# The silu behind a layer norm written to PSUM instead of SBUF, and an output projection whose first pass covers three column tiles instead of four

## The reference, cut to what matters

```
a, gl, z = split(u @ w_in, 3)
v = a * sigmoid(gl)
y = depthwise_conv(v, width 31) + b_dw
y = silu(layernorm(y, g_ln, b_ln))       # mean and variance over the 1024 channels
out = (y * silu(z)) @ w_out              # 1024 x 1024
h = h + rmsnorm(out, g_post)
```

## Time and profile before

| | us |
|---|---|
| median of 3 runs | 633.22 |
| lowest and highest run | 632.15, 635.92 |
| the profiled execution's own time | 633.14 |
| its span, first to last instruction | 631.4 |
| busy over the span: PE, DVE, ACT, POOL | 545.7, 451.3, 306.8, 298.2 |

### The profile page before, as it was taken

The page is one execution under the profiler, slowest core; times in us unless marked ns, Lnnn a source line. Parts: engine busy times, 40 slices in busy tenths (PEclk is TensorE's granted clock), DMA queues, the critical chain, the costliest instruction groups (busy, mean ns, idle before and its releaser), DMA issues.

```text
span 631.4 us, 10827 instructions
## 1 busy us (share of the span) xinstructions
PE 545.7 (86%) x4044; PEld 497.4 (79%) x4044; DVE 451.3 (71%) x855; ACT 306.8 (49%) x730; POOL 298.2 (47%) x271
## 2 busy tenths in 40 slices
PE   0699999999983669998999998998999999779981
PEld 0699999988952669987999997777777777469980
DVE  4887999999987994888758122856867868850066
ACT  5454665365646773655336325355454554444230
POOL 3349878898894770473647731102111112205033
PEclk9999999999997689999999999999999999959996
DMA  7233133222430310332133222020030031101003
GB/s 239 82 104 89 52 103 90 79 76 66 136 86 1 103 31 28 88 95 67 34 101 105 95 83 57 15 72 17 13 91 2 17 120 36 49 17 51 2 30 112
DMA packets 31397, 43.17 MB, mean 68 GB/s; under 512 B 5840, under 2 KB 21744, under 8 KB 31344
## 3 DMA queue, kind: packets, MB, share of 16 engines
q1 hardware_dynamic: 31344, 42.47, 23.2%
HBM read 37.25 MB, written 3.10 MB: 64 GB/s over the span
## 4 chain that ended last, share of the span: by engine, by line
PE 42%; DVE 36%; ACT 6%; issue 5%; POOL 4%; SPq 3%; DMA 3%; DVEq 0%; ACTq 0%; POOLq 0%
DVE ps L957 13%; PE ps L421 10%; PE ps L423 9%; PE ps L422 9%; PE ps L1636 3%; PE ps L1677 2%; DVE probs L1209 2%; POOL part L1288 2%; DVE y L1002 2%; PE ps L1657 2%; DVE ps L871 2%; SPq L484 2%; ACT probs L787 2%; POOL rlow_lo L412 1%; DVE y L854 1%
## 5 line engine op out<-in xcount | busy, mean ns | idle before, releaser
L412 POOL TENSOR_TENSOR rlow_lo<-stage,rlow_hi 128x384 fp32r<-128x384 f32 (+2 forms) x88 | 99.6, 1141 | 215.8 <-ACT rlow_hi L406 215.8
L421 PE MATMUL ps<-act_hi,rlow_hi 128*128 128x272 f32 (+1 forms) x368 | 110.7, 301 | 22.0 <-POOL act_lo L1341 9.3
L957 DVE SCALAR_TENSOR_TENSOR ps<-v,vecs,ps 128x574 f32<-128x574 f32 x165 | 120.6, 814 | 0.0
L421 PE MATMUL ps<-act_hi,rtop_hi 128*128 128x272 f32 x384 | 112.8, 294 | 7.7 <-ACT zs L627 4.0
L423 PE MATMUL ps<-act_hi,rtop_lo 128*128 128x272 f32 x384 | 111.7, 291 | 0.0
L422 PE MATMUL ps<-act_lo,rtop_hi 128*128 128x272 f32 x384 | 111.3, 290 | 0.0
L423 PE MATMUL ps<-act_hi,rlow_lo 128*128 128x272 f32 (+1 forms) x368 | 107.9, 293 | 0.0
L422 PE MATMUL ps<-act_lo,rlow_hi 128*128 128x272 f32 (+1 forms) x368 | 107.8, 293 | 0.0
L421 PEld LDWEIGHTS ps<-act_hi,rlow_hi 128*128 128x128 f32 (+1 forms) x368 | 70.4, 191 | 25.6 <-POOL act_lo L1341 10.6
L421 PEld LDWEIGHTS ps<-act_hi,rtop_hi 128*128 128x128 f32 x384 | 73.0, 190 | 9.1 <-ACT zs L627 4.3
L412 POOL TENSOR_TENSOR rtop_lo<-stage,rtop_hi 128x384 fp32r<-128x384 f32 (+1 forms) x56 | 64.8, 1177 | 28.4 <-ACT rtop_hi L406 28.4
(11 more groups left out here) (180 smaller groups left out, 1254.9 us busy)
## 6 DMA issues: line engine op xcount, KB each, us to landing
stage<-w_in SPq DMA_DIRECT2D x64, 192.0 KB, 2.7
stage<-w_bi SPq DMA_DIRECT2D x24, 256.0 KB, 2.7
stage<-w_ao SPq DMA_DIRECT2D x16, 256.0 KB, 2.9
stage<-w_bo SPq DMA_DIRECT2D x16, 256.0 KB, 2.7
stage<-w_qb SPq DMA_DIRECT2D x16, 192.0 KB, 2.6
xT<-x_t SPq DMA_DIRECT2D x4, 544.0 KB, 5.5
y_out<-xT SPq DMA_DIRECT2D x16, 136.0 KB, 1.8
stage<-w_kb SPq DMA_DIRECT2D x8, 256.0 KB, 2.6
```

The costliest lines, as they stand in the source:

```text
L412: nc.gpsimd.tensor_tensor(l, stage[:, u % STAGES, 0:unit_cols(u)], h.bitcast(F32), ALU.subtract).then_inc(lo_done, 1)
L421: nc.tensor.matmul(out, wh, xh, start=start, stop=False)
L957: ins = nc.vector.scalar_tensor_tensor(out=dst, in0=src, scalar=tap, in1=dst, op0=ALU.mult, op1=ALU.add)
```

## The change

The silu writes into one of two PSUM banks, taken in turn, and the gate reads it there; its other operand (`zs`) and its output (`y`) stay in SBUF. The banks are 6 and 3 in block 0 and 6 and 7 in block 1. The silu of step n waits for the gate of step n - 2, which read the bank before. Bank 6 is no longer free for the reciprocal of block 1, so both blocks use bank 5, and the second reciprocal waits until the eight normalisations of block 0 are done. Bank 3 is no longer free for output tile 3 during the first pass, so this pass covers tiles 0 to 2 (nine matmuls for each k), and tile 3 comes behind it as a tile of its own, without a wait for an evacuation.

```
-LNB = (5, 6)
+LN_RSTD = 5
+SILU_BANKS = ((6, 3), (6, 7))
+O_FIRST = 3
...
+        def silu_out(n):
+
+            b, k = divmod(n, KD)
+            return ps[:, SILU_BANKS[b][k % 2], 0:HB]
...
                 act.wait_ge(ln_norm, n + 1)
-                nc.scalar.activation(y[:, k, blk(b)], y[:, k, blk(b)], ACT.Silu, bias=vecs[:, V_BLN + k:V_BLN + k + 1],
+                if n >= 2:
+                    act.wait_ge(yz_full, n - 1)
+                nc.scalar.activation(silu_out(n), y[:, k, blk(b)], ACT.Silu, bias=vecs[:, V_BLN + k:V_BLN + k + 1],
...
-                bank = {N_IN: 4, N_IN + 1: 5, N_LN: LNB[0], N_LN + 1: LNB[1], N_O[0]: 4, N_O[1]: 5,
+                bank = {N_IN: 4, N_IN + 1: 5, N_LN: LN_RSTD, N_LN + 1: LN_RSTD, N_O[0]: 4, N_O[1]: 5,
...
-                nc.vector.tensor_tensor(y[:, k, blk(b)], y[:, k, blk(b)], zs[:, k, blk(b)], ALU.mult).then_inc(yz_full, 1)
+                nc.vector.tensor_tensor(y[:, k, blk(b)], silu_out(n), zs[:, k, blk(b)], ALU.mult).then_inc(yz_full, 1)
...
                 if n == KD:
+                    dve.wait_ge(ln_norm, KD)
                     inverse(N_LN + 1, None, 1)
...
-                for m in range(4):
+                for m in range(O_FIRST):
...
-            for n in range(4, 2 * KD):
+            for n in range(O_FIRST, 2 * KD):
                 b, m = divmod(n, KD)
-                pe.wait_ge(o_evac, n - 3)
+                if n >= 4:
+                    pe.wait_ge(o_evac, n - 3)
```

## The result

The changed kernel takes **630.63 us** (median of 17 runs, 628.33 to 632.33). The kernel before takes 635.76 (17 runs in all, with the three known earlier; 631.89 to 637.27). The ratio is 0.9933, with a 95% interval of 0.9918 to 0.9949: faster by 0.5 to 0.8%. The medians lie 5.13 apart; the forecast was a gain of 4.87.

The account below looks back on a forecast made before the run. DVE's gate and POOL were taken to hold each other up, leaving PE idle before tile 4. Gains of 3.25 (tile 4's earlier start) and 1.62 (clock) sum to 4.87 off 633.14, giving 628.3; range 626.0 to 631.5.

Parts of the forecast that it names:

- The gate reads PSUM: DVE's sixteen gates: each falls from 1.02 to 0.43 us, the centring's time, shedding 9.4 on DVE, not itself the gain.
- POOL late next, 1.99 a step: POOL in block 0: rests shorten by 0.2, steps go from 2.19 to 1.99, the eighth rest ends 1.6 earlier.
- The first pass over three tiles: PE's output projection: pass ends at 224.9, tile 3 then takes 3.02 alone, a price covered by PE's wait for bank 0.
- Tile 4's wait and the clock: PE at output tile 4: starts at 227.9 instead of 231.15, gaining 3.25; without the clock's fall, a further 1.62.
- the dip: Granted clock falling to 1.2 GHz behind PE's idle gap before tile 4; its removal was priced at 1.62.
- Silu into PSUM and the new waits: ACT's silu writes and the added waits: taken as costing nothing; the write's bounds were -0.05 to +0.22 each.
- The lead carried on: From tile 5 to the end: all of the lead is passed on; the other bound was that it is lost.
- The rival of the thinner pass: PE's clock falls in the nine-matmul pass: tile 3 cold costs 2.4, gain 2.5, 630.7; chance 0.14.
- How the numbers follow: Chances for the whole run: 0.16 faster by over one per cent (6.3 us), 0.81 within it, 0.03 slower.
- one dip fewer: Rival: arriving earlier at later low-clock stretches avoids one more dip, worth 1.62, giving 626.7; chance 0.14.
- the low clock: Rival: clock falls in the thinner pass (gain 2.5) or the old dip returns at tile 4 (gain 3.25); chance 0.14.
- The base: Starting time of the forecast: profiled execution's 633.14, 0.08 below the median of 633.22.

Follow-up runs that it names:

- e3: Kernel before with only the gate's second operand changed, to a reciprocal already in PSUM, leaving silu(z) out of the result: 626.25 us, ratio 0.9883.
- e6: e4 with every odd rest (low part of y) moved from POOL to DVE: 631.13 us, ratio 0.9949 to the kernel before.
- e7: e4 with the tail's scaling on DVE taken through PSUM: 621.34 us, ratio 0.9785 to the kernel before.
- e4: Changed kernel with one silu bank instead of two and four tiles in the first pass again: 627.45 us, ratio 0.9895 to the kernel before.
- e8: e4 once more, unedited, on the chip of e5 to e7: 627.31 us, ratio 0.9871 to the kernel before.
- e5: Changed kernel with one silu bank instead of two, first pass still over three tiles: 629.24 us, ratio 0.9916 to the kernel before.
- e2: Kernel before with only the first pass cut to three tiles, silu and gate left in SBUF: 632.89 us, ratio 0.9971.
- e1: The changed kernel run again with no edit, for a second profile: 630.01 us, ratio 0.9935 to the kernel before.

## Why the prediction was right, and where it was wrong

*The gate reads PSUM: right.* 0.437 where 0.43 was said. e3 shows that the operand alone does it, e6 and e7 that it holds for other instructions and in both directions. One reading was off: the rest that takes 0.76 at 230.60 does not run beside fewer gates. A gate starts inside it, at 230.68, and takes 0.98. What spared this rest is that it began first (see the last section). The Trainium skill, "SBUF — State Buffer", section "Who interferes with whom", says that a DVE instruction with two SBUF inputs contends with a GpSimd instruction that reads SBUF, and that one with at most one SBUF input, outside the two-port modes, does not. The trace agrees: 1020 ns against 437 for the gate, and 0.97 against 0.77 for the rest beside it.

*POOL late next, 1.99 a step: right.* Measured 1.97; the eighth rest ended 0.17 sooner than said. e6 supports it: where every second rest is taken off POOL, the last rest of block 0 ends 1.0 sooner.

*The first pass over three tiles: right in its price.* Tile 4 followed at 18.87 behind the first rest; 18.94 was said (227.9 - 208.96). The sentence that PE's wait for bank 0 covers this price described the kernel before. With the gate repaired no such wait is left: in e4, with four tiles and `evac_o(0)` at 227.09, PE does not wait for it. The prediction took the three tiles as given and did not ask what the gate alone would bring. That is 2.6 more (e4 and e8 against e5).

*Tile 4's wait and the clock: right.* No idle time ahead of tile 4, 1.00 from 218 on, 3.32 and a further 1.57 up to tile 6's evacuation (3.25 and 1.62 were said). e2 separates the two: 1.54 for the dip alone.

*Silu into PSUM and the new waits: right.* 0.577 on average against 0.607, so the write costs nothing, as taken. The row of 0.38 that served as a copy from PSUM for its lower bound is the square (line 626); the sum does not use it. e4 and e5 wait even more strictly at no cost.

*The lead carried on: right as far as it can be seen.* 4.89 at tile 6 and 4.88 at attention's start (4.79 in e1). At the tail's table load it is 5.00 in the profile after (395.99 and 390.99 behind the first rest) and 3.87 in e1's (392.12): there the scatter of the stretch between is as large as what is looked for. The medians lie 5.13 apart, and 4.40 in e1.

*The rival of the thinner pass: fell.* Four of the eight groups of nine put it to the test. The first four ran at the low clock from the start and left PE no wait, as the prediction says of a cold pass. Ahead of each of the last four PE idled 0.46 to 0.59, and the clock stayed at 1.00 from 218 on; in e1 and e5, with idle times of 0.56 to 0.59, it stayed there too. By the Trainium skill, "TensorE: Matmul & The Clock Gate", section "A second HAM failure mode: psum-queue depth-cycling", short idles between groups can make it swing; here four in a row did not.

*How the numbers follow: this is the step that failed.* The time and its cause were as forecast, and the ratio of 0.9933 lies within one per cent, the case that had 0.81. But the text called one per cent, 6.3 us, about what a measurement of this kernel can tell from no change, and so its likeliest case read as a change that makes no difference. The runs say otherwise: the interval of 0.9918 to 0.9949 is 1.0 us to either side, and the whole of it lies on the faster side. A gain of 5.13 is there and can be told from none, although it is less than one per cent. Even e2, 1.5 us below, could be told from no change (0.9951 to 0.9991). With that bound the chance of a gain that can be seen was the forecast's 0.59 (4.87 us), 0.14 (one dip fewer, 6.5) and 0.14 (the low clock, 2.5 to 3.25): 0.87 in place of 0.16. The bound of 6.3 was a round share of the time, six times what the repeated runs leave open and more than the spread of the three runs on hand (632.15 to 635.92); it had not been set against the size of the move.

*The base.* The forecast of 628.3 lies 2.3 below the 630.63 measured, although the gain was right within 0.3. The three runs' median of 633.22 was 2.5 below that of all 17, and the base was taken from them; for that reason the result lies above the forecast's own 627.5 to 630.0, though inside the whole range. Two short series of sums that take 2.56 to 4.90 and 2.1 to 3.7 from one profile to the next, and the 229.45 to 232.99 from attention's start to the tail, are of that size; that they make the scatter of the runs was not measured.

## What to carry to other kernels

Where DVE and POOL work at once, look for DVE instructions with both inputs in SBUF that take longer beside POOL than alone, and let the step ahead of them write one operand to PSUM; both engines get quicker. Test such a repair by itself before anything is rearranged around it: here the second half of the change gave back 2.6 us of what the first had won, and the same repair in the tail was worth another 6.0. And price a gain against the interval that repeated runs give, not against a round share of the time, and don't take the base from three runs.

## What the runs showed that was not expected

The granted clock of a short series of matmuls can differ between two executions of one program with the same idle time ahead: in the kernel after the sums of y had 0.50 in one profile and 1.00 in the next, both behind 2.08 of idle time, and the last sums took 3.74 and 2.10 behind 2.32. That was worth 2.1 and 1.6 us, so a difference of that size between two single profiles of this kernel can be that alone. It is no rare event here: with about the same idle time ahead, the sums of y ran at the high clock throughout in three of the ten profiles (before, e1, e7), and the last sums in four of nine (before, e1, e4, e5).

Contention between DVE and POOL costs both, and what each pays follows from which began first. DVE's gate goes from 0.44 to 1.02 on average, POOL's rest from 0.77 to 0.97. But the 1.02 is a mean of two kinds. In the kernel before, eleven of the sixteen gates start inside a POOL instruction with 0.5 or more of its time still to run; they take 0.85 to 1.57, and every one ends 0.29 to 0.30 behind the end of that instruction, as if it did its work once POOL was done. The other five take 0.43 or 0.44: no POOL instruction runs, or the gate began first or together with one, or within 0.1 of one's end. A POOL instruction that starts beside a running gate is the one that pays, by up to 0.3. DVE's order of time in the kernel before:

```profile
223.81 0.85 DVE L1002 TENSOR_TENSOR y<-y,zs 128x272 f32<-128x272 f32 x1
```

POOL's:

```profile
222.81 1.55 POOL L412 TENSOR_TENSOR rtop_lo<-stage,rtop_hi 128x512 fp32r<-128x512 f32 x1
```

This weight unit starts 0.05 behind a gate (222.76, 0.43 long) and takes 1.55 where the others take 1.27 to 1.30; it ends at 224.36, and the next gate, which started at 223.81 inside it, ends at 224.66. The pair of the earlier trace rows shows the same (213.40 and 213.70), and so does the rest on DVE in e6 (near 217.1, and 217.33).
